# In a gated feed-forward layer, one sum is made in PSUM: ScalarE seeds a bank, TensorE adds onto it

## What is computed

```
def _swiglu(h, w_in, w_out):
    g, u = jnp.split(h @ w_in, 2, axis=-1)
    return (jax.nn.silu(g) * u) @ w_out

x = x + 0.5 * mod[:, :, 2] * _swiglu(modulated(0, x), ffn_w_in[l, 0], ffn_w_out[l, 0])
```

## Time and profile before

| | |
|---|---|
| median of three runs | 2334.97 us |
| span of the profiled execution, first to last instruction | 2332.0 us |
| granted clock of TensorE | 1.000 of full speed |
| TensorE matmul busy | 2315.6 us, 99% |
| VectorE busy | 1570.3 us, 67% |
| ScalarE busy | 949.1 us, 41% |
| chain that ended last, share of TensorE | 91% |

### The profile page before, as it was taken

One profiled execution on the slowest core, in us unless ns is written; L12 is line 12 of the kernel. 1 busy time (PEld: TensorE's weight loads), 2 busy tenths in 40 slices (PEclk: granted clock), 3 DMA queues, 4 the chain that ended last, 5 costly groups with the idle time before them and its releaser, 6 DMA issues.

```text
span 2332.0 us, 39464 instructions
## 1 busy us (share of the span) xinstructions
PE 2315.6 (99%) x16468; PEld 2236.7 (96%) x16468; DVE 1570.3 (67%) x2385; ACT 949.1 (41%) x1491; POOL 30.6 (1%) x44
## 2 busy tenths in 40 slices
PE   8999999999999999999999999999999999999999
PEld 8999999989789999999999999999999999999999
DVE  6886776658867876776587777676245768467473
ACT  5433423444656523414364243245215355234142
POOL 0000000000001000000010000000000010000000
PEclk9999999999999999999999999999999999999999
DMA  9352544422101344334224344225221012322132
GB/s 301 127 163 96 190 148 145 166 70 64 48 19 55 105 149 140 114 109 156 86 91 157 115 156 152 85 78 173 90 73 46 19 55 73 109 73 91 56 99 73
DMA packets 203194, 251.58 MB, mean 108 GB/s; under 512 B 13106, under 2 KB 180874, under 8 KB 203018
## 3 DMA queue, kind: packets, MB, share of 16 engines
q1 hardware_dynamic: 202594, 248.89, 32.5%
q10 hardware_dynamic: 424, 0.18, 0.0%
HBM read 245.76 MB, written 3.28 MB: 107 GB/s over the span
## 4 chain that ended last, share of the span: by engine, by line
PE 91%; DVE 3%; ACT 2%; DMA 2%; issue 1%; SPq 1%; POOL 0%; DVEq 0%; ACTq 0%
PE banks L1111 80%; PE banks L1264 1%; PE banks L1443 1%; PE banks L1442 1%; PE banks L1441 1%; DMA w_raw<-ffn_w_in 1%; PE banks L1588 1%; PE banks L1600 1%; PE banks L1615 1%; DMA mod_first<-w_mod 1%; SPq L1072 0%; SPq L879 0%; PE banks L1809 0%; DVE w_lo L2658 0%; ACT w_hi L2041 0%
## 5 line engine op out<-in xcount | busy, mean ns | idle before, releaser
L1111 PE MATMUL banks<-b_hi,w_hi 128*128 128x320 f32 x2496 | 775.8, 311 | 2.9 <-DVE b_lo L2833 1.2
L1111 PE MATMUL banks<-b_hi,w_lo 128*128 128x320 f32 x2496 | 771.2, 309 | 0.0
L1111 PE MATMUL banks<-b_lo,w_hi 128*128 128x320 f32 x2496 | 771.2, 309 | 0.0
L1111 PEld LDWEIGHTS banks<-b_hi,w_hi 128*128 128x128 f32 x2496 | 468.5, 188 | 15.8 <-issue 9.6
L2041 ACT ACTIVATE w_hi<-w_raw 128x1024 fp32r<-128x1024 f32 x296 | 310.4, 1056 | 403.2 <-PE banks L1111 228.9
L1111 PEld LDWEIGHTS banks<-b_lo,w_hi 128*128 128x128 f32 x2496 | 468.6, 188 | 0.0
L1111 PEld LDWEIGHTS banks<-b_hi,w_lo 128*128 128x128 f32 x2496 | 468.6, 188 | 0.0
L2658 DVE TENSOR_TENSOR w_lo<-w_raw,w_hi 128x1024 fp32r<-128x1024 f32 x296 | 361.4, 1223 | 152.1 <-ACT w_hi L2041 150.6
L1111 PE MATMUL banks<-hid_hi,w_hi 128*128 128x320 f32 x1664 | 400.1, 311 | 0.5 <-DVE hid_lo L2962 0.5
L1111 PE MATMUL banks<-hid_lo,w_hi 128*128 128x320 f32 x1664 | 396.2, 309 | 0.0
L1111 PE MATMUL banks<-hid_hi,w_lo 128*128 128x320 f32 x1664 | 396.2, 309 | 0.0
(11 more groups left out here) (343 smaller groups left out, 2409.6 us busy)
## 6 DMA issues: line engine op xcount, KB each, us to landing
w_raw<-ffn_w_in SPq DMA_DIRECT2D x176, 512.0 KB, 4.8
mod_grain<-w_mod SPq DMA_DIRECT2D x78, 512.0 KB, 6.0
w_raw<-ffn_w_out SPq DMA_DIRECT2D x64, 512.0 KB, 4.4
last_grain<-w_mod SPq DMA_DIRECT2D x40, 512.0 KB, 5.2
w_raw<-ffn_w_out SPq DMA_DIRECT2D x32, 384.0 KB, 3.6
w_raw<-w_in_odd SPq DMA_DIRECT2D x20, 512.0 KB, 4.7
mod_first<-w_mod SPq DMA_DIRECT2D x6, 1024.0 KB, 11.8
w_raw<-w_in_even SPq DMA_DIRECT2D x12, 512.0 KB, 5.8
```

The source lines that it names most:

```text
L1111: ins = pe.matmul(o, w3[w], v3[v][cols], start=first and i == 0, stop=last and i == 2, skip_group_check=onto_read)
```

## The change

P1 is no longer copied to SBUF. ScalarE copies it from bank A into bank B (`keep_p1`), and the products of P2 are added on top of it: item 2 no longer has a start flag, so it accumulates. The bank then holds C11. A new ScalarE instruction, `silu_c11`, reads that bank, applies Silu and writes `work[:, s, 0]`. The later Silu covers C12 alone. VectorE's `add_p2` is gone.

The waits follow. TensorE's item 2 waited for the products of the double before it (`prod_done`) and now waits for P1's copy, once for each hidden tile. P1's copy waited for `hid_lo` of the double before, because it wrote `work`; now it waits for `prod_done`. Item 4's wait for P1 is gone. Item 0 of the next double waited for the addition in bank B and now waits for the Silu that reads it. VectorE's product waits for both Silus.

```diff
-        ITEM_STARTS = (True, True, True, False, False, False, False)
+        ITEM_STARTS = (True, True, False, False, False, False, False)
@@ free_parts (TensorE)
-                        pe.wait_ge(c11_done, done)
+                        pe.wait_ge(c11_silu, done)
-                elif t == 2:
-                    pe.wait_ge(prod_done, 22 * f + 2 * d)
                 elif t == 3:
                     pe.wait_ge(p5_kept, done + 2)
-                elif t == 4:
-                    pe.wait_ge(p1_kept, done + 2)
@@ free_part (TensorE)
+                elif t == 2:
+                    pe.wait_ge(p1_kept, n)
@@ keep_p1 (ScalarE)
-                n = 22 * f + 2 * d + s
                 part_done(f, d, 0, s)
-                act.wait_ge(hid_lo_done, n - 1)
-                act.activation(work[:, s, 0, :], role(d, s, "A"), ACT.Copy).then_inc(p1_kept, 1)
+                act.wait_ge(prod_done, 22 * f + 2 * d)
+                act.activation(role(d, s, "B"), role(d, s, "A"), ACT.Copy).then_inc(p1_kept, 1)
+
+            def silu_c11(f, d, s):
+
+                part_done(f, d, 2, s)
+                act.wait_ge(hid_lo_done, 22 * f + 2 * d + s - 1)
+                act.activation(work[:, s, 0, :], role(d, s, "B"), ACT.Silu).then_inc(c11_silu, 1)
@@ double (ScalarE)
                 if not last and d > 2:
                     item_hi(f, d + 1, 0)
                 for s in range(2):
+                    silu_c11(f, d, s)
+                for s in range(2):
                     keep_u2(f, d, s)
...
-                    act.activation(work[:, s, 0:2, :], work[:, s, 0:2, :], ACT.Silu).then_inc(silu_done, 1)
+                    act.activation(work[:, s, 1, :], work[:, s, 1, :], ACT.Silu).then_inc(silu_done, 1)
@@ VectorE
-            def add_p2(f, d, s):
-
-                part_done(f, d, 2, s)
-                dve.wait_ge(p1_kept, pairs_before(f, d) + s + 1)
-                dve.tensor_tensor(work[:, s, 0, :], work[:, s, 0, :], role(d, s, "B"), ALU.add).then_inc(c11_done, 1)
-
@@ double (VectorE)
-                for s in range(2):
-                    add_p2(f, d, s)
                 item_lo(f, d, 6)
...
                 for s in range(2):
+                    dve.wait_ge(c11_silu, done + s + 1)
                     dve.wait_ge(silu_done, n + s + 1)
```

More of the change, by code:

```diff
@@ L179, in trunk @@
         u2_kept = sem("u2_kept")
-        c11_done = sem("c11_done")
+        c11_silu = sem("c11_silu")
         c12_done = sem("c12_done")
```

## The result

| | before | after |
|---|---|---|
| median, 21 runs of each | 2334.38 us | 2338.16 us |
| ratio of the times, 95% interval | | 1.0016 [1.001, 1.0023] |
| span of the profiled execution | 2332.0 us | 2336.0 us |
| span of a second profiled execution | 2331.7 us | 2335.9 us |

The changed kernel is 3.8 us slower. The forecast was 6.0 us slower, 2341.0 us, with 0.62 on slower by more than 0.2% (4.7 us). The median lies inside that bound, at 0.16%. The same two kernels once more, 26 runs of the one and 11 of the other, gave 1.0019 [1.001, 1.0028]. Both intervals leave out 1: that the kernel is slower is measured, that it is slower by 0.2% is not.

The account below looks back on a forecast made before the run. TensorE, 99% busy, was taken as the bound. Stops at item 2 (5.85 us), late U2 (0.3) and an old wait gone (-0.15) gave 6.0 us on the 2334.97 us median: 2341.0 us, range 2336.0 to 2346.5.

Parts of the forecast that it names:

- The lateness of P1's copy: TensorE's item 2 stops for P1's copy in doubles 1 to 3; 5.85 us net over the four FFNs.
- The view: Expected row of TensorE's waits for ScalarE's bank-to-bank copy: eight to ten entries, near 4.5 us, longest 0.8 to 1.0.
- What VectorE's free time does: Without the additions of P2, the weight sum and loads leading to P1 in double 2 come 0.79 us earlier.
- The swallowed wait: Second FFN, double 1: an existing TensorE wait before item 6 swallows 0.67 of the 0.88 us stop; 0.21 stays.
- the term for TensorE's old waits: Of TensorE's old waits, item 6 waiting for C22 (1.2 us in 4 places), one may go: -0.15 us.
- U2 behind the Silus: ScalarE's new Silus ahead of U2 delay it in four doubles whose split came late from its load: 0.3 us.
- The copy's own cost: ScalarE's copy into PSUM taken as 0.42 to 0.44 us; ends 0.278 and 0.709; quicker PSUM access might save 1.7 us.
- Full payment: Rival, chance 0.12: all eleven latenesses at item 2 count as traced, 10.7 us, giving 2345.7 us.
- Only double 1: Rival, chance 0.20: the chain to P1 in doubles 2 and 3 moves forward enough; 3.0 us, giving 2338.0 us.
- The relief: Rival, chance 0.10: P1's copy starts earlier and VectorE's free time removes TensorE's old waits; not slower, 2333.5 to 2335 us.
- the write to PSUM: Rival, chance 0.06: ScalarE's copy into PSUM is slow, 2.4 us on top of the forecast, giving 2343.4 us.
- P2's products did add onto what ScalarE had written: Rival, chance 0.02, claimed the opposite: P2 does not add onto the copy; values change, time stays 2341.0 us.

Follow-up runs that it names:

- the kernel with the wait alone: Kernel before, VectorE's additions kept, with each half of TensorE's item 2 also waiting for P1's copy: 2341.18 us against 2333.55, ratio 1.0032.

## Why the prediction was right, and where it was off

**What bounds the kernel** held: TensorE is busy for 99% of both spans, and VectorE's time fell from 67% to 66% for nothing that shows in the total.

**The lateness of P1's copy** held, but for one place. Ten stops, all in doubles 1 to 3: 1.20, 0.18 and 0.19 us in the first FFN, 0.79, 0.90 and 0.19 in the second, 0.79 in the third, 0.79, 0.84 and 0.19 in the fourth. Each has 0.07 behind it, and the sum is 6.06 + 0.70 = 6.8 us, for 6.5 forecast (6.72 in the table counts what the half items show). By the terms, each with its 0.07:

- Double 1: 0.86 in three FFNs for 0.88; 1.27 in the first for 1.00. The prediction counted back from U2 by five half items of 1.76 us, and in this double of the kernel before TensorE waited 0.27 us at item 3 in between. So item 2 had started at 66.01, not 66.29, and P1 was 1.20 late. The stop at item 2 then swallows those 0.27 us at item 3 (most of the -0.33 of the table), in the kernel with the wait alone too, and the two errors cancel in the sum.
- Double 2: 0.97 in the second FFN for 1.13, 0.91 in the fourth for 0.61 (1.19 in the second profile), 0.25 in the first for 0.28, none in the third, as said. The loads in the chain to P1 took another time than in the profile read: in the fourth FFN the second of them 4.88 and 5.16 us for 4.68.
- Double 3: 0.26 for 0.27, three times.

**The view** counted six waits and 4.3 us, for 8 to 10 and 4.5: the four stops under 0.2 us are hidden in the 0.31 us of a matmul. The longest is 1.0, in double 1 of the first FFN, not double 2 of the second. Against item 0, item 2 of that double 2 starts 0.90 us later, for the 1.3 that I had named; the 1.3 didn't agree with my own term of 1.13.

**What VectorE's free time does** held where it was priced. The weight sum behind double 1 starts at 775.68, 23.29 us after item 0 of that double (752.39); before it was 776.06 - 751.83 = 24.23. That is 0.9 us earlier, for 0.8.

```profile
775.68 1.23 DVE L2684 TENSOR_TENSOR w_raw<-w_raw 128x1024 f32<-128x1024 f32 x1 [0.62 <-DMA w_raw<-ffn_w_in]
```

Against the kernel with the additions and the wait the loads are issued 0.79 us earlier at two stops, which is the term.

**The swallowed wait** held as a mechanism, but the profile after does not show it. Item 6 of the second FFN's double 1 waited 0.59 + 0.07 and doesn't wait any more, but its load was also 0.85 us shorter (4.80 for 5.65), which alone would have ended the wait. The kernel with the wait alone separates the two: its load took 0.47 us longer (6.12), and item 6 still waited only 0.27 us with what follows it: 0.66 + 0.47 - 0.86 = 0.27.

**The step that was off is the term for TensorE's old waits**, "one may go, -0.15 us of the earlier trace rows". Item 6 gave back 2.1 us in both pairs of profiles, of which 0.67 and 0.73 were the swallowed wait: 1.4 us, nine times my term. 0.58 us of that in the first pair is the chance of one load; the rest, 0.8 us there and 1.6 in the second pair, where that load went the other way by 0.2, points to VectorE's free time for about half and is open for the other half. I read them off one profile as four entries of 1.2 us in all. That view leaves out the part that a matmul's duration hides: by starts, item 6 waited 2.7 us. And such waits wander from execution to execution with the loads. A further 0.3 us went at item 3, swallowed as said, and 0.45 ahead of the first double, which the kernel before shows by itself in its second profile. Last, the median of three runs that I started from was 0.6 us above that of 21: this alone puts 2341.0 that much too high. (The 3.0 us between the time and the span of the kernel before compare two executions: nearly every run on record is about 1.8 us above its own span.)

**U2 behind the Silus**: 0.1 and 0.3 us in the two profiles, for 0.3, in double 9 of the first FFN rather than in double 5 of the fourth.

**The copy's own cost.** P1's copy averages 405 ns from bank to bank, and 434 from bank to SBUF before:

```profile
L2241 ACT ACTIVATE banks<-banks 128x320 f32<-128x320 f32 x80 | 30.4, 405 | 15.8 <-PE banks L1111 15.8
```

The first of a pair, on which the stops hang, lasts 0.42 us in both the earlier trace rows; only the second is shorter (0.39 in the mean for 0.44). So neither end of my bounds was near. The Trainium skill's rule (ScalarE: Activation LUTs, "Step-by-step: what each stage is for", PSUM as the lower-latency destination) fits the mean of the 80, by 29 ns. The estimate of 0.186 us less for each stop is not borne out.

**The rivals.** Full payment asked for stops of 10.7 us, and even with VectorE's additions kept the kernel paid 7.6, so it would have been too high even then. Only double 1 was to pay 3.0 us: its 2338.0 is near the measured time, but by chance, since doubles 2 and 3 stopped for 2.9 us. The relief did not win, and the write to PSUM is not slow. P2's products did add onto what ScalarE had written; matmuls had written that bank before, so nothing here tells what a bank would do that none had written. The chances were too high for slower: 0.42 of 0.50 of my forecast lay above the bound, which left little for a relief that I could not read.

## What to carry to other kernels

A wait moved forward onto an engine's copy costs what that engine's queue has ahead of the copy: look for the instruction that it stands behind, and what that one waits for. Here nine of ten stops vanished when the copy was put ahead of one split, and the time was then that of the kernel before within its interval (1.0002 [0.9993, 1.0011]), as an engine busy for 66% had promised. Where the bound engine also has small waits on loads, take a second profile before pricing them: one of them differed by 0.9 us between two executions of one kernel, and the change at hand is 3.8.

## What the runs showed of the hardware

- A packet of TensorE's instructions (16 KB, 130 in the span) delays a weight load of 512 KB that it falls into. Of the second loads of a pair in all 14 profiles, the 52 with a packet 1 to 3.8 us behind the issue took 6.53 us in the median and never under 5.77; the 292 with one later than that took 4.94, and the 672 with none near 4.97. A few dozen instructions more at the head of the program moved a wait 770 us later from 1.67 to 0.60 and 0.18 us.
- Behind a stop of 2.09 us TensorE's granted clock was 0.50 in the stretch from 1962 to 1964 and 0.70 in the next 2 us, and that cost 1.5 us. One profile shows it, and two of that kernel's five executions have a mean clock under 1.000; behind stops of 1.43 to 1.75 us in other kernels the clock stayed at 1.00.
- TensorE starts 0.14 to 0.15 us after the end of the copy that it waits for (760.22 against 760.08, 785.83 against 785.68), with the copy's result in PSUM as with an addition's in SBUF (0.15).
